# Two transformer layers and a third block on one core: layer boundaries rebuilt tile by tile, gate columns computed inside the layer, context first

## Chip, core and metric

One core of one Trainium2 chip, device time in microseconds (us), everything in fp32. Engines: PE (TensorE), DVE (VectorE), ACT (ScalarE), POOL (GpSimd), SP (SyncE, which here only issues the weight transfers). The change is judged by the median of three runs.

## What is computed

The input x has 256 tokens of 1024 numbers. Two layers follow that share their form, then a block of another form with a mixture of 16 experts. Cut to the parts that matter here:

```python
for l in range(2):                                   # the two layers
    shift, scale, gate = split3(silu(c) @ w_ada[l] + b_ada[l])
    h = rms_norm(x, g_pre[l]) * (1 + scale) + shift
    y = sum of three gated attention branches over h, then @ w_out[l]
    x = x + gate * rms_norm(y, g_post[l])
# second block: shift1, scale1, gate1, shift2, scale2, gate2 = silu(c_2) @ w_mod_2 + b_mod_2
h  = rms_norm(x,   g_pre1_2) * (1 + scale1) + shift1
hc = rms_norm(ctx, g_pre1_2) * (1 + scale1_ctx) + shift1_ctx     # 256 context tokens
x = x + gate1 * rms_norm(windowed and recurrent attention over hc and h @ w_out_2, g_post1_2)
x = x + gate2 * rms_norm(sum over experts e of scatter(w_down[e] @ act(w_gate[e], w_up[e])), g_post2_2)
```

Shift, scale and gate are called the columns: each is a vector of 1024 numbers per condition, made from 4 MB of weights in six pieces of 512 for one layer (pieces 0 to 3 are shift and scale, 4 and 5 the gate).

## The kernel before

The kernel is written by hand: each engine has its own instruction stream, and semaphores count what is done. Work on PE is a list of **jobs**, each of which fills one of three PSUM banks in turn (job j uses bank j mod 3); the next user of a bank waits until ACT or DVE has read it (`reader`, `free`, `taken`). `layer_jobs` and `second_jobs` are these lists, in order. Weights come through a ring of 6 slots of 1 MB, filled by SP in the order of `layer_loads` and `second_loads`. A load waits for the last job that uses the load six places ahead of it, and SP issues strictly in order.

Jobs that the text names. `xT`, `xT2`, `cT`: transposes of normalised x or context, evicted with scale and shift into hT or hcT by ACT (even) and DVE (odd). `ada`, `mod`: 512 columns of a conditioning product; `modT`: their turn onto partitions, after an ACT copy, reduced by DVE. `gate`: gate columns spread over partitions, read by DVE into G1. `cq`, `ckv`, `qb`, `kb` and so on: projections of hT. `wo`, `wout`: output projections; wout has four jobs of 8 products of 128x512, two for each tile of 128 tokens. In the second block `tq`, `tk`, `tkc` are queries, keys and context keys, `rq`, `rk` the rotations of q and k, `nv` values.

Order of a layer: 4 xT, 3 gate, cq ckv qb kb, small projections; 24 attention units, between which the *fill* jobs (z, g, ada, modT) are spread by `share`; 12 wo; 4 wout. Then the **boundary**: DVE copies the four wout banks to SBUF, ACT squares the copies, DVE and POOL make the inverse root, DVE scales by G1 and adds to x for both tiles, ACT issues three small loads (lvecs, b_ada, g_post) and squares x, POOL makes the root, DVE normalises both tiles, and PE transposes. The columns for layer l+1 are made in the fill of layer l, all six pieces, and those for layer 0 in the prologue, ahead of the loop (`FIRST_MODS`). The two layers are one hardware loop (`Fori`). Ahead of the prologue's columns PE computes bias tables (L711, L715), which go to DRAM and come back skewed (t_rows, na_rows). The second block starts with loads of context, constants (consts2) and gate rows once x is done.

The experts' weights, 16 times about 33 MB, stream through a ring of 13 slots; at the end ACT squares the four output tiles, DVE scales, adds, and SP stores x.

## Time and profile before

| | us |
|---|---|
| median of 3 runs | 2490.72 (2490.24 to 2492.41) |
| profiled execution, its own time | 2487.14 |
| its span, first to last instruction | 2484.7 |
| PE busy | 1887.4 (76%) |
| DVE busy | 511.9 (21%) |
| ACT busy | 284.8 (11%) |
| DMA | 714.89 MB, mean 288 GB/s |

Busy shares are means over stages of different kinds; PE's weight loads (PEld) overlap its products. A row of a timeline merges neighbouring instructions of one line, and the brackets at its end give the idle time of the engine before it and what ended that.

### The profile page before, as it was taken

Reading aid. Unit: us, or ns where it says so; the run is one execution under the profiler, and the core shown is the slowest. Engines: PE = TensorE matmul, PEld = TensorE weight load, DVE = VectorE, ACT = ScalarE, POOL = GpSimd, SP = SyncE. Lnnn points to the kernel's source line nnn. Section 1 sums busy time; section 2 is a strip of 40 time slices with the busy share of each in tenths; the row PEclk is TensorE's granted clock in tenths of the full one; section 3 lists DMA queues with packets and bytes.
Section 4 is the critical chain, followed back from the end, with each engine's and each line's share of the span. In section 5 each row is a group of like instructions: output and inputs, shape, how many; then the busy total and the mean of one; then the engine's idle time right before and its main releaser. Section 6 shows DMA issues by size and latency. Waiting matters only on the chain.

```text
span 2484.7 us, 25429 instructions
## 1 busy us (share of the span) xinstructions
PE 1887.4 (76%) x10486; PEld 1043.9 (42%) x10486; DVE 511.9 (21%) x1131; ACT 284.8 (11%) x699; POOL 53.1 (2%) x80
## 2 busy tenths in 40 slices
PE   5899999799999699977656666666666666666665
PEld 1767776668777567533412222222222222222221
DVE  1224322224322226743300000000000000100001
ACT  1112220113220112311100000000000000000000
POOL 0000000000000300020000000000000000000000
PEclk9999999899999899999788878887788788878787
DMA  9633563233554411156599999999999999999996
GB/s 322 185 136 107 199 220 120 85 131 141 198 182 163 154 68 68 68 179 240 243 423 422 422 422 423 422 422 421 423 423 422 422 423 423 421 423 422 423 423 274
DMA packets 149549, 714.89 MB, mean 288 GB/s; under 512 B 11711, under 2 KB 16191, under 8 KB 95904
## 3 DMA queue, kind: packets, MB, share of 16 engines
q1 hardware_dynamic: 143776, 697.08, 70.0%
q0 software_dynamic: 2016, 7.21, 1.2%
q10 hardware_dynamic: 3640, 8.94, 1.1%
q8 instruction: 86, 1.41, 0.2%
q14 instruction: 31, 0.25, 0.0%
HBM read 709.38 MB, written 3.80 MB: 287 GB/s over the span
## 4 chain that ended last, share of the span: by engine, by line
issue 64%; PE 29%; DVE 4%; DMA 2%; ACT 1%; POOL 0%; ACTq 0%; POOLq 0%; DVEq 0%
PE banks L756 10%; PE banks L1539 3%; PE banks L1548 3%; PE banks L761 1%; PE banks L810 1%; PE banks L1584 1%; PE banks L1569 1%; PE banks L876 1%; DVE arena L2015 1%; PE banks L819 1%; PE banks L715 1%; PE banks L904 1%; DMA arena<-in_w_mods_dram 1%; PE banks L886 1%; DVE arena L1945 1%
## 5 line engine op out<-in xcount | busy, mean ns | idle before, releaser
L2231 PE MATMUL banks<-arena 128*32 128x512 f32 (+2 forms) x3072 | 468.1, 739 | 307.0 <-DMA arena<-in_w_up_dram 301.1
L2231 PEld LDWEIGHTS banks<-arena 128*32 128x32 f32 x3072 | 128.5, 136 | 587.4 <-issue 580.8
L756 PE MATMUL banks<-arena 128*128 128x256 f32 x1536 | 344.8, 382 | 1.4 <-DVE arena L1253 1.4
L756 PEld LDWEIGHTS banks<-arena 128*128 128x128 f32 x1536 | 289.3, 191 | 43.0 <-DVE arena L1253 3.2
L2258 PE MATMUL banks<-arena 128*32 128x512 f32 x1280 | 212.9, 803 | 114.6 <-DMA arena<-in_w_down_dram 75.5
L2370 DVE SCALAR_TENSOR_TENSOR arena<-arena,banks 64x512 f32<-64x512 f32 (+1 forms) x48 | 30.5, 635 | 787.9 <-ACT arena L2283 787.2
L2258 PEld LDWEIGHTS banks<-arena 128*32 128x32 f32 x1280 | 46.7, 132 | 261.5 <-issue 260.1
L2283 ACT ACTIVATE arena<-banks 64x512 f32<-64x512 f32 (+1 forms) x48 | 26.6, 555 | 837.6 <-PE banks L2231 831.7
L1539 PE MATMUL banks<-arena 128*128 128x256 f32 x512 | 113.4, 380 | 0.2 <-DVE arena L1880 0.2
L1539 PEld LDWEIGHTS banks<-arena 128*128 128x128 f32 x512 | 96.3, 191 | 12.9 <-DVE arena L1880 0.4
L2377 DVE COPY arena<-banks 128x512 f32<-128x512 f32 x16 | 11.1, 692 | 369.1 <-PE banks L2266 369.1
L848 PE MATMUL banks<-arena 128*128 128x256 f32 x384 | 83.4, 380 | 1.3 <-DVE arena L1349 1.3
L848 PEld LDWEIGHTS banks<-arena 128*128 128x128 f32 x384 | 73.0, 191 | 11.8 <-issue 2.2
L1548 PE MATMUL banks<-arena 128*128 128x512 f32 x160 | 69.7, 594 | 1.1 <-DVE arena L1909 1.1
L2203 PE MATMUL banks<-arena 128*128 128x512 f32 x128 | 60.9, 619 | 0.8 <-ACT arena L2297 0.8
L2235 PE MATMUL banks<-arena 128*32 128x128 f32 x512 | 60.2, 316 | 0.0
L856 PE MATMUL banks<-arena 128*128 128x512 f32 x128 | 55.4, 594 | 3.1 <-issue 3.1
L2235 PEld LDWEIGHTS banks<-arena 128*32 128x32 f32 x512 | 37.7, 133 | 36.7 <-issue 21.8
L2297 ACT COPY arena<-banks 128x512 f32<-128x512 f32 x16 | 9.4, 585 | 344.7 <-PE banks L2266 344.7
L2214 PE MATMUL banks<-arena 64*128 64x64 f32 x176 | 30.4, 296 | 21.7 <-DVE arena L2372 13.0
L1051 ACT ACTIVATE arena<-arena 128x256 f32<-128x256 f32 x64 | 32.0, 500 | 125.6 <-DVE arena L1275 67.0
L1548 PEld LDWEIGHTS banks<-arena 128*128 128x128 f32 x160 | 30.2, 191 | 37.9 <-issue 36.0
(316 smaller groups left out, 1657.9 us busy)
## 6 DMA issues: line engine op xcount, KB each, us to landing
arena<-in_w_gate_dram SPq DMA_DIRECT2D x128, 1376.0 KB, 30.1
arena<-in_w_up_dram SPq DMA_DIRECT2D x128, 1376.0 KB, 31.9
arena<-in_w_down_dram SPq DMA_DIRECT2D x160, 1024.0 KB, 30.4
arena<-in_w_in_dram SPq DMA_DIRECT2D x68, 1024.0 KB, 7.2
arena<-in_w_mods_dram SPq DMA_DIRECT2D x48, 1024.0 KB, 7.3
arena<-in_w_out_dram SPq DMA_DIRECT2D x12, 1024.0 KB, 5.1
arena<-in_w_down_dram SPq DMA_DIRECT2D x16, 512.0 KB, 21.7
arena<-in_w_o_swa_dram SPq DMA_DIRECT2D x4, 1024.0 KB, 10.5
```

Source lines behind the costliest of these rows:

```text
L756: mm = pe.matmul(b[:, i * S:i * S + S], w, rhs[:, kt, :], start=kt == 0, stop=kt == 7)
L848: mm = pe.matmul(b[:, i * S:i * S + S], w[:, k, c:c + P], zv[:, 4 * br + k, :], start=k == 0, stop=k == 3)
L856: mm = pe.matmul(b, hTv[:, kt, t * P:t * P + P], slot(loads[0] + kt // 4)[:, kt % 4, :], start=kt == 0, stop=kt == 7)
L1051: ins = nc.scalar.activation(Ev[:, u % 3, t * S:t * S + S], src, ACT.Exp, bias=nmx[:, u % 3, t:t + 1], scale=QK ** -0.5 if kind == "mla" e ...
L1539: mm = pe.matmul(b[:, i * S:i * S + S], slot(loads[kt // 4])[:, kt % 4, c0:c0 + P], rhs[:, kt, :], start=kt == 0, stop=kt == 7)
L1548: mm = pe.matmul(b, lhs[:, kt, (n % 2) * P:(n % 2) * P + P], slot(loads[kt // 4])[:, kt % 4, :], start=kt == 0, stop=kt == 7)
L2203: mm = pe.matmul(acc[2 * t + c], GT[:, e % 2, t * P:t * P + P], Y[:, 512 * c:512 * c + 512], start=e == 0, stop=e == NE - 1, skip_group_ch ...
L2214: mm = pe.transpose(MB[:, b:b + 64], hid[0:64, c], ident[0:64, 0:64])
L2231: mm = pe.matmul(bank[pc][32 * g:32 * g + 32, 0:w_], xsT[:, kt, CAP * e4:CAP * e4 + CAP], (wg if g < 2 else wu)[:, c:c + w_], start=kt == ...
L2235: mm = pe.matmul(bank[pc][32 * g:32 * g + 32, LAST - c0:w], xsT[:, kt, CAP * e4:CAP * e4 + CAP], (wg if g < 2 else wu)[:, FF - 64:FF].unsq ...
L2258: mm = pe.matmul(bank[c][32 * g:32 * g + 32, :], hTv3[:, j, 32 * hf:32 * hf + 32], w_[:, 512 * c:512 * c + 512], start=(g, c) not in start ...
L2370: nc.vector.scalar_tensor_tensor(h_, h_, 1.0, bank[pc][0:64, 0:w], ALU.add, ALU.mult).then_inc(own3.sem, own3.up())
```

## The change

At each boundary y stays in PSUM: ACT squares the wout banks directly, DVE scales them from PSUM by a G1 that already holds the factor 0.5, and each tile of 128 tokens goes its own way, from the sum of squares to the transposes. wout runs tile by tile. Shift and scale of the next stage are computed in the fill as before (4 pieces instead of 6); the gate's two pieces are loaded and computed inside the layer they belong to, and in the second block inside that. Gate jobs move among the middle projections. Small loads of the next stage are issued after the last attention unit, in the last layer also those of the context, which is squared and normalised there. The second block starts with context keys. In the prologue the constants load first, table products stand between column products, and the layers are unrolled. At the end scaling, addition and stores go by tile and half.

```diff
@@ layer_loads, layer_jobs @@
     chunk("w_in", D, COL["qb"], 512)
+    for c in (4, 5):
+        chunk("mods_now", D, 512 * c, 512)
     chunk("w_in", D, COL["kb"], 256)
...
-    for c in range(3):
-        jobs.append(("gate", c, ()))
...
-    jobs += [("qb", 0, (i, i + 1)), ("qb", 1, (i, i + 1))]
-    i += 2
+    jobs += [("qb", 0, (i, i + 1)), ("ada", 4, (i + 2, i + 3)), ("qb", 1, (i, i + 1)), ("ada", 5, (i + 4, i + 5)), ("modT", 4, ())]
+    i += 6
...
-    for c in range(2):
-        jobs += [("wout", 2 * c, (i, i + 1)), ("wout", 2 * c + 1, (i, i + 1))]
-        i += 2
+    for t in range(2):
+        jobs += [("wout", 2 * t + c, (i + 2 * c, i + 2 * c + 1)) for c in range(2)]
+    i += 4
@@ prologue @@
-FIRST_MODS = [("ada", 0), ("ada", 1), ("modT", 0), ("ada", 2), ("modT", 1), ("ada", 3), ("modT", 2), ("ada", 4),
-              ("modT", 3), ("ada", 5), ("modT", 4), ("modT", 5)]
+FIRST_MODS = [("ada", 0), ("ada", 1), ("modT", 0), ("ada", 2), ("modT", 1), ("ada", 3), ("modT", 2), ("modT", 3)]
@@ second_loads, second_jobs @@
-ORDER2 = ("qn", "kn", "vn", "qh", "zf", "zb", "gh", "ih")
+ORDER2 = ("kn", "vn", "qn", "qh", "zf", "zb", "gh", "ih")
...
-    jobs = [("xT2", i, ()) for i in range(4)] + [("cT", i, ()) for i in range(4)]
-    jobs += [("gate2", i, ()) for i in range(3)]
+    jobs = [("cT", i, ()) for i in range(4)]
...
+    jobs += [("tkc", n, i["kn"]) for n in range(2)]
+    jobs += [("xT2", n, ()) for n in range(4)]
+    jobs += [("own", 4, i["own", 4]), ("own", 5, i["own", 5])]
+    jobs += [("tk", n, i["kn"]) for n in range(2)]
+    jobs += [("ownT", 4, ()), ("ownT", 5, ())]
+    jobs += [("nv", n, i["vn"]) for n in range(2)] + [("gate2", n, ()) for n in range(3)]
+    jobs += [("rk", n, ()) for n in range(2)] + [("nv", n, i["vn"]) for n in (2, 3)]
+    jobs += [("tq", n, i["qn"]) for n in range(2)] + [("rq", n, ()) for n in range(2)]
@@ PE @@
-            with pe.Fori(0, LAYERS) as l:
+            for l in range(LAYERS):
@@ ACT, end of a layer @@
+                for t in range(2):
+                    for c in range(2):
+                        n = 2 * t + c
+                        j = JOB_OF["wout", n]
+                        act.wait_ge(job_done.sem, made(l, j))
+                        nc.scalar.activation(E[:, 512 * n:512 * n + 512] if n < 3 else th[:, 0:512], bank[j % BANKS], ACT.Square,
+                                             scale=0.5, accum_out=s4[:, n:n + 1]).then_inc(ysq.sem, ysq.up())
+                    act.wait_ge(xup.sem, xup.at(l, t + 1))
+                    nc.scalar.activation(xnv[:, t, :], xv[:, t, :], ACT.Square, accum_out=xss[:, t:t + 1]).then_inc(xsq.sem, xsq.up())
@@ DVE, end of a layer @@
-                for t in range(2):
-                    nc.vector.scalar_tensor_tensor(xnv[:, t, :], xnv[:, t, :], rs[:, t:t + 1], G1, ALU.mult, ALU.mult).then_inc(v_own.sem, v_own.up())
+                    for c, j in enumerate(js):
+                        a = slice(512 * c, 512 * c + 512)
+                        nc.vector.scalar_tensor_tensor(xnv[:, t, a], bank[j % BANKS], rs[:, t:t + 1], G1[:, a],
+                                                       ALU.mult, ALU.mult).then_inc(reader(j), 1)
...
+                    nc.vector.tensor_tensor(xv[:, t, :], xv[:, t, :], xnv[:, t, :], ALU.add).then_inc(xup.sem, xup.up())
+                    x_mean(l + 1, t)
+                    x_scale(l + 1, t)
```

What stands on PE at the start, before (L711 and L715 are the bias tables, L729 the column products, L735 their turns):

```order
L711 MATMUL banks<-arena 12x512
L715 MATMUL banks<-arena 120x512 x8
L729 MATMUL banks<-arena 32x512 x16
L735 MATMUL banks<-arena 128x128 x4
L729 MATMUL banks<-arena 32x512 x8
```

and after (L751 column products, L757 turns, L761 and L740 tables, L818 xT, L789 cq and ckv):

```order
L751 MATMUL banks<-arena 32x512 x16
L757 MATMUL banks<-arena 128x128 x4
L761 MATMUL banks<-arena 12x512
L740 MATMUL banks<-arena 120x512 x4
L751 MATMUL banks<-arena 32x512 x8
L757 MATMUL banks<-arena 128x128 x4
L740 MATMUL banks<-arena 120x512 x4
L751 MATMUL banks<-arena 32x512 x8
L757 MATMUL banks<-arena 128x128 x8
L818 MATMUL banks<-arena 128x128 x16
L789 MATMUL banks<-arena 128x256 x24
```

The tables moved behind the first column products, two column products and two turns are gone, and nothing stands between xT and cq.

DVE at the end of layer 0, before (L1385 scales by G1, L1387 adds to x, both on whole tiles):

```order
L1382 TENSOR_SCALAR arena<-arena 128x2
L1383 REGISTER_ALU
L1385 SCALAR_TENSOR_TENSOR arena<-arena 128x1024
L1386 REGISTER_ALU
L1387 TENSOR_TENSOR arena<-arena 128x1024
L1385 SCALAR_TENSOR_TENSOR arena<-arena 128x1024
L1386 REGISTER_ALU
L1387 TENSOR_TENSOR arena<-arena 128x1024
```

and after (L1468 scales from PSUM, L1472 adds, L1210 and L1214 are the mean and the normalising of x for the next layer, L1255 evicts xT):

```order
L1461 TENSOR_TENSOR arena<-arena 128x1
L1463 TENSOR_SCALAR arena<-arena 128x1
L1468 SCALAR_TENSOR_TENSOR arena<-banks,arena 128x512 x2
L1472 TENSOR_TENSOR arena<-arena 128x1024
L1210 TENSOR_SCALAR arena<-arena 128x1
L1214 TENSOR_SCALAR arena<-arena 128x1024
L1461 TENSOR_TENSOR arena<-arena 128x1
L1463 TENSOR_SCALAR arena<-arena 128x1
L1468 SCALAR_TENSOR_TENSOR arena<-banks,arena 128x512 x2
L1472 TENSOR_TENSOR arena<-arena 128x1024
L1210 TENSOR_SCALAR arena<-arena 128x1
L1214 TENSOR_SCALAR arena<-arena 128x1024
```

The steps of one tile now follow each other, up to its normalising, before those of the next.

PE at the start of the second block, before (L1527 xT2 and cT, L1520 gates, L1539 projections of keys and queries, L1544 rotations, L1548 nv, L1603 first scores):

```order
L1527 MATMUL banks<-arena 128x128 x32
L1520 MATMUL banks<-arena 128x128 x8
L1539 MATMUL banks<-arena 128x256 x96
L1544 MATMUL banks<-arena 128x512 x4
L1548 MATMUL banks<-arena 128x512 x32
L1603 MATMUL banks<-arena 128x256 x4
```

and after (L1620 cT, L1633 projections, L1611 xT2, L1592 own columns, L1599 their turns, L1642 nv, L1605 gates, L1638 rotations, L1698 first scores):

```order
L1620 MATMUL banks<-arena 128x128 x16
L1633 MATMUL banks<-arena 128x256 x32
L1611 MATMUL banks<-arena 128x128 x16
L1592 MATMUL banks<-arena 32x512 x16
L1633 MATMUL banks<-arena 128x256 x32
L1599 MATMUL banks<-arena 128x128 x8
L1642 MATMUL banks<-arena 128x512 x16
L1605 MATMUL banks<-arena 128x128 x8
L1638 MATMUL banks<-arena 128x512 x2
L1642 MATMUL banks<-arena 128x512 x16
L1633 MATMUL banks<-arena 128x256 x32
L1638 MATMUL banks<-arena 128x512 x2
```

The first scores come next there, so the rotations of q are the last work ahead of them; before, the values were.

## Rows read from the trace of the kernel before

**Rows 1.** The page: tenths busy and GB/s in 40 slices of the span.
```profile
PE   5899999799999699977656666666666666666665
GB/s 322 185 136 107 199 220 120 85 131 141 198 182 163 154 68 68 68 179 240 243 423 422 422 422 423 422 422 421 423 423 422 422 423 423 421 423 422 423 423 274
```

**Rows 2.** Stretches: length, busy (count) of PE, PEld, DVE, ACT, POOL, clock, DMA share, GB/s.
```profile
248.00:310.00 62.00, 60.31 (x331) 47.69 (x320) 22.53 (x68) 16.93 (x50) 2.79 (x4) 1.00 0.55 202
431.00:449.00 18.00, 0.89 (x3) 0.09 (x2) 8.48 (x15) 3.11 (x7) 1.39 (x2) 0.62 0.40 127
```

**Rows 3.** PE's waits up to 1290 us: total, times, longest.
```profile
PE banks L789 <- DVE arena L1188: 31.5, 2, 17.1
PE banks L1527 <- DMA arena<-in_consts_dram: 18.7, 1, 18.7
```

**Rows 4.** Timeline of PE, 0 to 90 us: start, duration, instructions, idle before.
```profile
10.05 1.88 PE L711 MATMUL banks<-arena 33*12 33x512 f32 x2 [10.05 <-DMA arena<-in_na_hot_dram]
11.85 14.00 PE L715 MATMUL banks<-arena 32*120 32x512 f32 x16
...
27.59 6.13 PE L729 MATMUL banks<-arena 128*32 128x512 f32 x32 [1.73 <-DVE arena L1151]
34.24 1.92 PE L729 MATMUL banks<-arena 128*32 128x512 f32 x16
...
68.77 3.68 PE L789 MATMUL banks<-arena 128*128 128x128 f32 x16 [14.43 <-DVE arena L1188]
75.06 14.19 PE L761 MATMUL banks<-arena 128*128 128x256 f32 x64 [0.21 <-DVE arena L1205]
```

**Rows 5.** DMA: page totals; windows 40:45, 20:25 (two rows), 16:28; issues, time to landing.
```profile
q1 hardware_dynamic: 143776, 697.08, 70.0%
q0 software_dynamic: 2016, 7.21, 1.2%
...
DMA packets 976, 1.93 MB, mean 387 GB/s; under 512 B 32, under 2 KB 32, under 8 KB 976
...
DMA packets 428, 1.01 MB, mean 203 GB/s; under 512 B 19, under 2 KB 19, under 8 KB 428
q1 hardware_dynamic: 342, 0.66, 34.2%
...
q1 hardware_dynamic: 1193, 2.38, 51.6%
...
t_rows<-arena POOLq DMA_DIRECT2D x1, 768.0 KB, 13.5
na_rows<-arena POOLq DMA_DIRECT2D x1, 1920.0 KB, 20.4
```

**Rows 6.** Timeline between the two layers, DVE and PE.
```profile
434.79 1.28 DVE L1385 SCALAR_TENSOR_TENSOR arena<-arena 128x1024 f32<-128x1024 f32 x1
...
448.92 3.68 PE L789 MATMUL banks<-arena 128*128 128x128 f32 x16 [17.11 <-DVE arena L1188]
454.83 14.19 PE L761 MATMUL banks<-arena 128*128 128x256 f32 x64 [0.44 <-DVE arena L1205]
```

**Rows 7.** Timeline of PE at the start of the second block.
```profile
832.02 3.74 PE L1527 MATMUL banks<-arena 128*128 128x128 f32 x20 [18.75 <-DMA arena<-in_consts_dram]
...
837.70 2.05 PE L1520 MATMUL banks<-arena 128*128 128x128 f32 x16 [0.18 <-DVE arena L1867]
839.95 41.71 PE L1539 MATMUL banks<-arena 128*128 128x256 f32 x192 [0.20 <-DVE arena L1880]
```

**Rows 8.** The same timeline, from the values to the first scores.
```profile
886.93 27.73 PE L1548 MATMUL banks<-arena 128*128 128x512 f32 x64 [1.05 <-DVE arena L1909]
915.44 1.14 PE L1603 MATMUL banks<-arena 64*128 64x256 f32 x8 [0.78 <-ACT arena L1683]
```

**Rows 9.** Issue to landing of the second block's weight loads of 1 MB (L1488).
```profile
DMA to landing us min/median/max: 5.0/7.4/11.6
```

**Rows 10.** Timeline at the end: the last scatter.
```profile
2469.04 3.67 PE L2203 MATMUL banks<-arena 128*128 128x512 f32 x8 [0.84 <-ACT arena L2297]
```

More of the change, by code:

```diff
@@ L1120, in _ @@
             pool.dma_start(scr_na, EN[0:120, :]).then_inc(na_out, 16)
-            pool.wait_ge(const_in, 32)
-            minus_half = C("half")
-            with pool.Fori(0, LAYERS) as l:
+            for l in range(LAYERS):
                 enter("pool", l)
@@ L1237, in _ @@
                 dve.wait_ge(reader(j), taken(l, j))
+                columns(5)
+                dve.wait_ge(rows_in, 32 * l + 32)
                 for kind, n, _ in MIDDLE:
-                    if kind not in ("kc", "rotq"):
+                    if kind not in ("kc", "rotq", "gate"):
                         continue
@@ L1242, in _ @@
                     dve.wait_ge(job_done.sem, made(l, j))
+                    if kind == "gate":
+                        a = slice(3 * P * n, min(D, 3 * P * n + 3 * P))
+                        nc.vector.tensor_tensor(row_b[:, a], bank[j % BANKS][:, 0:a.stop - a.start], row_b[:, a], ALU.add).then_inc(v_own.sem, v_own.up())
+                        dve.wait_ge(v_own.sem, v_own.last())
+                        nc.vector.scalar_tensor_tensor(G1[:, a], row_b[:, a], 0.5, row_g[:, a], ALU.mult, ALU.mult).then_inc(reader(j), 1)
+                        continue
                     if kind == "kc":
@@ L1330, in _ @@
                         if kind == "modT":
[L1331 to L1333 removed]
+                            columns(n)
                         if kind == "z":
@@ L1530, in job @@
                     ctx_ = kind == "tkc" or (kind in ("zf", "zb") and n < 2)
-                    if kind == "tq" and n == 0:
-                        for jj in range(JOB2["xT2", 3] - 2, JOB2["xT2", 3] + 1):
+                    if kind in ("tkc", "tk") and n == 0:
+                        for i in range(4):
+                            jj = JOB2["cT" if kind == "tkc" else "xT2", i]
                             pe.wait_ge(reader(jj), taken(L2, jj))
@@ new lines, in _ @@
+            for n in range(2):
+                j = JOB2["tkc", n]
+                dve.wait_ge(job_done.sem, made(L2, j))
+                nc.vector.tensor_copy(kc2[:, 512 * n:512 * n + 512], bank2(j)).then_inc(reader(j), 1)
+            for t in range(2):
+                j = JOB2["xT2", 2 * t + 1]
+                dve.wait_ge(job_done.sem, made(L2, j))
+                for i in range(4):
+                    ins = nc.vector.tensor_scalar(hTv[:, 4 + i, t * P:t * P + P], bank2(j)[:, i * P:i * P + P],
+                                                  AB1[0][:, 12 + i:13 + i], AB1[0][:, 4 + i:5 + i], ALU.mult, ALU.add)
+                ins.then_inc(reader(j), 1)
```

574 lines of the change are left out of this document (309 added, 265 removed).

## Prediction, made blind

> **What bounds the kernel now.** I read the page first: TensorE (PE) is busy in nine tenths or more of most slices of the first half, and from slice 21 on the DMA engines are full at 422 GB/s while PE falls to six tenths [rows 1]. The stretch table says the same: in 248 to 310 us, an attention stage, PE works 60.31 of 62 us [rows 2]. The second half is a stream of expert weights of fixed size, so it is neither lengthened nor shortened: whatever is won before it moves it earlier by as much. The first half pays one for one wherever PE waits, and the list of PE's waits gives the places: 31.5 us in two waits of the transposes L789, 18.7 us in one of L1527 [rows 3]. These are the boundaries the change rewrites. The timeline says how they are made. At the start PE runs table products and the columns' products until 54 us, then idles 14.4 us, and the first real projection (cq, L761) starts at 75.06 [rows 4]. Between the layers PE has ended 17.11 before it transposes at 448.92, so at 431.8, and reaches cq at 454.83: 23.0 us [rows 6]. Before the second block it has ended 18.75 before 832.02, at 813.3, and starts tq at 839.95: 26.7 us [rows 7].
>
> **Start.** The four loads and two products for gate columns leave the prologue, the table products fill PE's gaps, small loads and gates leave its path. Two limits remain. PE alone: about 10 us until constants are in (estimated from 10.05, where the first table product could start), two column products 6.1, two more 2 x 1.92, four turns of columns 2.6, table products 1.9 + 14.0, transposes 3.7, a last eviction about 1.2 [rows 4]: 43. The transfers: before cq 8.4 MB of column weights, 1.7 MB of w_in and 2.35 MB of small loads must land, 12.5 MB. The undisturbed rate is 1.93 MB in 5 us, 387 GB/s; while the bias tables are written the weights get 0.66 MB in 5 us [rows 5]. In the 13.5 us that this write takes to land [rows 5] the weights move 1.8 MB, the remaining 10.7 take 27.6 us, start-up 2.5: 43.6. But the skewed reads and the na_rows write, which came after 63 us, now start as the last table product ends, about 37 us. At the shared rate of 198 GB/s (2.38 MB in the 12 us from 16 to 28 [rows 5]) the 2.9 MB then outstanding take 15 us: 51. Because cq starts on the first half of its weights I take **48** (bounds 43 and 52): 75.1 - 48 = **27** us gained.
>
> At the rate question stands the Trainium skill, DMA: Bandwidth & Descriptors, section Queues, rings and completion order: each DMA engine takes turns between queues, a packet at a time. With mean packets of 4.85 KB (weights) and 3.58 KB (tables), from the page's queue totals [rows 5], weights would keep 58% of 387, 222 GB/s, cq would be bound by PE at 44 and the whole sum would be 4 us lower. This speaks for the change, as a rival below. The row shows 131 with the total down to 203 GB/s [rows 5], so here the measurement does not agree.
>
> **Inside each layer.** PE's work is the same: six column products before, two for this layer and four for the next after. The fill between attention units gets shorter by 5.2 us (products 2 x 1.92 [rows 4], turns about 0.66 each), at no cost as long as PE is what bounds there (60.31 of 62 [rows 2]); were VectorE's chain the bound, up to 5 us per layer would not come back. The gates' 2.0 us [rows 7] move from the boundary into the middle: -2.0 per layer. A load waits for the last user of its slot, six loads back, and SP issues in order: kb's weights now wait for qb 1. 1 MB, which is what kb's two loads hold, landed after 5.0 us at best [rows 9]; covered by ada 5 (1.92 [rows 4]) and some 1.7 for a turn and the spread of the root, it leaves **1** us (0 to 3) per layer. In the first layer the own column weights (4 MB) arrive while the tables travel: **2** us (0 to 8). Start in all: 27 - 2 - 1 - 2 = **22**.
>
> **Between the layers.** Tile 0's chain runs under wout 2 and 3, each as long as a job nv (27.73 for four [rows 8]: 6.9). Tile 1's remains after PE's end. In 431 to 449 us VectorE worked 8.48, ScalarE 3.11 and POOL 1.39 us for both tiles [rows 2]. Of ScalarE's, 0.8 is the square of a quarter and 1.15 that of a tile: 2.0 remain. POOL's two roots remain, 1.4. Of VectorE's, the copy (0.7) goes and of scaling, addition and normalising (1.28 [rows 6], 1.2 and 0.75 a tile) one tile's remain, halved scaling costing 0.1 more: 3.3, with 0.6 of small steps. Hand-overs 0.6: 7.9 us. Then xT 2 and 3, 0.92 each at the low clock (3.68 for four [rows 6]), and the eviction in four pieces of 128x128, which no row has: the whole eviction of the four old jobs lay within the 5.9 us from 448.92 to 454.83, so it is below 2.2 (5.9 less 3.7), and not below 1.0 (half the columns of 0.5 for 128x256); I take 1.2 and 0.2 to start it, near the lower end, since the columns are halved: cq at +11.2. 23.0 - 11.2 = 11.8, less gates and kb: **8.8**. The granted clock after the wait was the low level (0.62 in the stretch table) [rows 2] and may be so again; included above.
>
> **Before the second block.** Context is normalised under wout. After PE's end: 7.9 of chain; then VectorE, in order, does the lbs steps (0.6) and the evictions of cT 1 and 3 (1.0 each): tkc starts at +10.7. From there to the first scores PE's work adds up: three pairs of projections (tkc, tk, tq; 64 of the 192 products in 41.71 each) 41.7; xT2 2.4, between the 3.68 of 16 transposes at the low clock and half of it; the own columns 3.8 and their turns 1.2; four jobs nv 27.7; gates 2.05; rotations 3.5 [rows 4, 7, 8]: 82.4. New waits: vn's two loads sit in kn's slots, and kn is used last by tk 1, so they issue only when that ends; the first lands 5.0 later at best [rows 9], with the two turns (1.2) as cover: **3.8** (3 to 7). Behind this wait stand nv, the gates and everything up to the scores. The rotations of q come last, so the first scores wait for six VectorE steps of 0.72 (3.7 beyond PE's own 1.7 and the hand-over), which nv used to cover: **3.7** (2 to 5). A bank that the gates hold costs 0.2. 10.7 + 82.4 + 7.7 = 100.8, against 915.44 - 813.3 = 102.2 now: **1.4**. So the 16 us that the shorter chain gives here go three ways: 5.0 for the columns moved in from the prologue (there they count as gained), 4.4 for xT2 and gates that stood in the old 26.7, and 5.3 net of waits (7.7 new, 2.4 old).
>
> **End.** Squares of the four tiles start as each product ends instead of after all (3.67 us for four) and the last square ends about 1.5 us earlier; the last transfer follows a 128x512 addition rather than 128x1024 (1.22 us) and is half as big. VectorE still does all of its closing work, about 5 us [rows 10]: **2.2**.
>
> **Sum.** 22 + 8.8 + 1.4 + 2.2 = 34.4. The profiled execution took 2487.1 us (span 2484.7), so 2452.7; it stood 3.6 below the runs' median 2490.7, which gives **2456** for the median.
>
> **Rivals.**
> - Table traffic or the own columns hold the start (12%): cq at 52 and 8 us of waits for own columns instead of 2: 10 us worse, 2466. For it: 20.4 us to land na_rows, 203 GB/s while tables travel [rows 5]. Against: the tables' own volume is the same as before, and most of the weights behind them have a stage of 14 us to arrive in.
> - The shorter fill is missed (8%): 5 us a layer do not come back, 2466. Against: PE idle of 1.7 us in 62 [rows 2].
> - The waits in the second block are longer and drop the clock (10%): 7 + 5 in place of 3.8 + 3.7, and 1.7 lost at the low level: 2462.
> - Everything hides, and the unrolled layers shed the register steps ahead of waits (17%): cq at 43, no wait for kb or own columns, 3 us of steps: 5 + 2 + 2 + 3, 2444.
> - The other side (2%): the two layers are unrolled, and PE's instructions are fetched instead of looped over. From 75 to 813 us are 738 us; it decides once PE there runs 34.4 us, or 4.7%, longer. At 10% it is 74 - 34 = 39 us slower than now, 2530. Against: the expert part is straight-line code already, and its DMA is full all the time [rows 1]. No change at all would need the same coincidence (1%).
> - Weights keep the larger share of the engines beside the tables (5%): 222 GB/s, by the packet sizes of the two queues, instead of 131 to 198. Then PE's own 44 binds cq: 4 better, 2452. It is the Trainium skill's rule above. Against: the measured 0.66 MB in 5 us [rows 5].
> - My forecast (45%), its own range 2449 to 2463.
>
> **Numbers.** Cases within reach run from 2444 to 2466; the single bounds reach further (cq's start -5 or +4, own columns +6, kb +4, fill +10, the second block's waits +5). Not all at once: 2442 to 2471. Faster by over 0.2% (5 us, about what can be told from no change) 0.97, the same 0.01, slower 0.02.
>
> **What would show it.** Right: cq at 44 to 52 us; PE's gap between layers in two pieces, together near 9 us instead of 17.1; tkc about 11 us after the last wout; a wait for w_in near 4 us at nv 0, one for VectorE near 4 us at the first scores, and 101 us from the last wout to them; the expert stage still at 422 GB/s and equally long. Wrong: over 8 us of waits for w_mods in layer 0, PE below 58 of 62 us in the attention stages, or a last stage that starts earlier but is longer.

## The result and the profile after

The changed kernel takes 2466.55 us in the median of 4 runs (2465.06 to 2471.28) against 2490.48 of before on the same chip (4 runs, 2489.96 to 2492.41): ratio 0.9906, 95% interval 0.9889 to 0.9923, 23.9 us faster. The forecast was 2456 against 2490.7, that is 34.4 faster; the size is 10 us short. The profiled execution has a span of 2463.2 us, 21.5 less than before. Of run 3 below one execution took 2941.10 us, at a mean granted clock of 0.63, and is left out of its median.

The start, PE's timeline (start, duration, instructions, idle before), to be read against [rows 4]:

```profile
9.56 1.94 PE L751 MATMUL banks<-arena 128*32 128x512 f32 x8 [9.56 <-DMA arena<-in_w_mods_dram]
17.87 1.94 PE L751 MATMUL banks<-arena 128*32 128x512 f32 x8 [6.37 <-DMA arena<-in_w_mods_dram]
20.69 1.94 PE L751 MATMUL banks<-arena 128*32 128x512 f32 x8 [0.89 <-DMA arena<-in_w_mods_dram]
23.31 1.94 PE L751 MATMUL banks<-arena 128*32 128x512 f32 x8 [0.68 <-DMA arena<-in_w_mods_dram]
...
26.22 1.88 PE L761 MATMUL banks<-arena 33*12 33x512 f32 x2
28.03 7.18 PE L740 MATMUL banks<-arena 32*120 32x512 f32 x8
35.13 3.64 PE L751 MATMUL banks<-arena 128*32 128x512 f32 x16
...
43.97 3.64 PE L751 MATMUL banks<-arena 128*32 128x512 f32 x16
...
54.06 14.17 PE L789 MATMUL banks<-arena 128*128 128x256 f32 x64 [1.66 <-DVE arena L1255]
...
79.19 1.07 PE L801 MATMUL banks<-arena 128*32 128x512 f32 x8 [0.59 <-DMA arena<-in_w_mods_dram]
81.78 1.06 PE L801 MATMUL banks<-arena 128*32 128x512 f32 x8 [1.52 <-DMA arena<-in_w_mods_dram]
```

The reader is to see that PE does nothing for 9.56 us and little until 20, waiting for column weights, and only at 26 begins the tables, whose inputs landed by 16 us at the latest (run 3 below). The first projection, L789, starts at 54.06 instead of 75.06. The products themselves are slow here: eight of L751 take 1.94 us, eight of L801, of the same form, 1.07 at 79.19. The clock column doesn't show this at first: it reads 1.00 for 35.1 to 38.7 us and 0.50 for 44.0 to 47.5, and 16 products take 3.64 us in both. So the durations decide. The list of PE's waits in the first 54 us sums it up (total, times, longest):

```profile
PE banks L751 <- DMA arena<-in_w_mods_dram: 17.5, 4, 9.6
```

The last of these waits ends at 23.31 us. The write of the table rows, the first of the table traffic, is issued by POOL only then:

```profile
37.15 0.90 POOL L1163 DMA_DIRECT2D t_rows<-arena  x1
```

Between the layers, where [rows 6] had one gap of 17.11 us:

```profile
387.71 27.70 PE L884 MATMUL banks<-arena 128*128 128x512 f32 x64 [1.77 <-DVE arena L1438]
...
417.99 0.65 PE L818 MATMUL banks<-arena 128*128 128x128 f32 x4 [2.14 <-DVE arena L1468]
422.85 1.94 PE L818 MATMUL banks<-arena 128*128 128x128 f32 x8 [4.21 <-DVE arena L1214]
```

The last wout ends at 387.71 + 27.70 = 415.41; the gap is now 2.14 (a bank that DVE still reads), 4.21 (the chain of tile 1) and 1.66 before cq, which starts at 426.45.

The second block, against [rows 7] and [rows 8]; L1620 is cT, L1633 the projections tkc, tk, tq, L1642 the values nv, L1698 the scores:

```profile
790.49 1.31 PE L1620 MATMUL banks<-arena 128*128 128x128 f32 x8 [2.14 <-DVE arena L1468]
794.57 1.12 PE L1620 MATMUL banks<-arena 128*128 128x128 f32 x4 [2.76 <-ACT arena L1774]
797.62 16.94 PE L1633 MATMUL banks<-arena 128*128 128x256 f32 x64 [1.94 <-DVE arena L1931]
...
820.76 14.08 PE L1633 MATMUL banks<-arena 128*128 128x256 f32 x64
...
840.51 15.67 PE L1642 MATMUL banks<-arena 128*128 128x512 f32 x32 [4.79 <-DMA arena<-in_w_in_dram]
...
860.19 13.89 PE L1642 MATMUL banks<-arena 128*128 128x512 f32 x32
...
893.33 2.08 PE L1698 MATMUL banks<-arena 64*128 64x256 f32 x8 [3.56 <-DVE arena L1984]
895.34 5.54 PE L1633 MATMUL banks<-arena 128*128 128x256 f32 x16
```

Two things are to be seen. The announced waits are there, 4.79 for vn's weights and 3.56 for VectorE before the first scores. And equal work differs in length: 64 products take 16.94 us behind the boundary and 14.08 later, 32 values 15.67 and 13.89, a score row 2.08 where [rows 8] has 1.14. The granted clock tells why (stretches; after the counts: clock, DMA share, GB/s):

```profile
422.00:432.00 10.00, 7.49 (x22) 6.04 (x23) 4.43 (x14) 2.21 (x7) 0.00 (x0) 0.53 0.06 20
432.00:440.00 8.00, 8.00 (x38) 6.62 (x37) 0.00 (x0) 0.77 (x2) 0.00 (x0) 1.00 0.00 0
794.00:804.00 10.00, 7.49 (x20) 5.91 (x21) 2.88 (x8) 1.43 (x4) 10.00 (x17) 0.53 0.37 126
893.00:900.00 7.00, 6.67 (x21) 5.11 (x22) 3.65 (x10) 0.81 (x2) 0.00 (x0) 0.57 0.30 113
```

0.53 means nearly all at the lower of the two levels (1.2 GHz), 1.00 the upper (2.4). PE had idled ahead of each low stretch: 4.21 and 1.66 us ahead of the first, 2.76 and 1.94 around the second, 3.56 ahead of the third.

The end: the squares of the four output tiles start as each product ends (2451.96 to 2454.54), where they had waited for all, and the span closes 12.37 us after the last scatter starts, in place of 15.66.

Stage by stage, in us, before and after from the same kinds of row; "won" is positive where the changed kernel is faster.

| stage | before | after | won | forecast |
|---|---|---|---|---|
| to cq of layer 0 | 75.06 | 54.06 | 21.0 | 27 |
| layer 0, cq to end of wout | 356.7 | 361.3 | -4.6 | -5 |
| end of wout to cq of layer 1 | 23.0 | 11.0 | 12.0 | 11.8 |
| layer 1, cq to end of wout | 358.4 | 361.5 | -3.0 | -3 |
| end of wout to first scores | 102.2 | 105.4 | -3.2 | 1.4 |
| first scores to the first expert product | 301.6 | 305.2 | -3.7 | 0 |
| expert products to the last scatter | 1252.1 | 1252.3 | -0.2 | 0 |
| last scatter to the end | 15.7 | 12.4 | 3.3 | 2.2 |
| sum (spans differ by 21.5) | | | 21.6 | 34.4 |

Three terms are short: the start by 6.0, the second block by 4.6, the stage behind it by 3.7, in all 14.3. The middle of the kernel came within 0.5 us a term, and the end gave 1.1 more. 14.3 less 1.1 and the small ones is the 12.8 that is missing in the sum. In medians 10.5 are missing: the profiled execution of before stood 3.6 us below its median, that of after 1.5.

### The profile page after: what moved, and what is told of

Same layout as the page of the kernel before. It is cut to its first block, busy times and chain, and to the rows that moved or that the text cites. A ratio compares the mean times of both kernels' runs of the same rounds, so it can differ in the third digit from the quotient of the medians.

```text
span 2463.2 us, 24454 instructions
## 1 busy us (share of the span) xinstructions
PE 1898.9 (77%) x10486; PEld 1042.2 (42%) x10486; DVE 510.6 (21%) x1148; ACT 287.7 (12%) x711; POOL 55.5 (2%) x86
## 4 chain that ended last, share of the span: by engine, by line
DMA 38%; PE 36%; DVE 5%; ACT 1%; issue 1%; SPq 1%; POOL 0%; DVEq 0%; ACTq 0%
DMA arena<-in_w_up_dram 33%; PE banks L784 7%; PE banks L2313 6%; DMA arena<-in_w_down_dram 4%; PE banks L1633 4%; PE banks L1642 3%; PE banks L2340 2%; PE banks L876 2%; PE banks L2282 2%; PE banks L1678 1%; PE banks L884 1%; PE banks L1663 1%; DVE arena L2090 1%; PE banks L2267 1%; PE banks L904 1%
## 5 line engine op out<-in xcount | busy, mean ns | idle before, releaser
L1633 PE MATMUL banks<-arena 128*128 128x256 f32 x512 | 118.5, 391 | 1.9 <-DVE arena L1931 1.9
L1633 PEld LDWEIGHTS banks<-arena 128*128 128x128 f32 x512 | 99.3, 197 | 17.9 <-issue 4.3
L1642 PE MATMUL banks<-arena 128*128 128x512 f32 x160 | 71.5, 605 | 4.8 <-DMA arena<-in_w_in_dram 4.8
L1642 PEld LDWEIGHTS banks<-arena 128*128 128x128 f32 x160 | 30.7, 194 | 42.2 <-issue 41.7
```

Source lines behind the costliest of these rows:

```text
L1633: mm = pe.matmul(b[:, i * S:i * S + S], slot(loads[kt // 4])[:, kt % 4, c0:c0 + P], rhs[:, kt, :], start=kt == 0, stop=kt == 7)
L1642: mm = pe.matmul(b, lhs[:, kt, (n % 2) * P:(n % 2) * P + P], slot(loads[kt // 4])[:, kt % 4, :], start=kt == 0, stop=kt == 7)
```

## The experiments

Two theories stood at the outset. **Serial start, uncovered waits, idle clock**: the start is PE's waits and work in series, the second block's two waits come from job order, and the low clock comes from PE's idling. **The rival**: transfers and table traffic bound the start, the load queue is late at vn anyway, and the low clock belongs to the place or the chip. Each run was timed beside the kernel before; medians over different chips are comparable to some 2 us (before stood at 2490.3 to 2492.3). Runs 1 to 4 were on one chip, 5 to 8 on a second, 9 to 11 on a third, 12 on a fourth; the changed kernel was timed only for the result. So "less than the changed kernel" carries these 2 us, and for runs 1, 5 and 9 the intervals of the ratios overlap its own (0.9889 to 0.9923): what these show is read from their rows.

### 1. tk ahead of the own column products

```diff
-    jobs += [("own", 4, i["own", 4]), ("own", 5, i["own", 5])]
     jobs += [("tk", n, i["kn"]) for n in range(2)]
+    jobs += [("own", 4, i["own", 4]), ("own", 5, i["own", 5])]
```

> The changed kernel with tk moved ahead of the layer's own column products in the second block, nothing else. Theory (the wait for vn's weights is the time from the end of tk 1 to the landing less what PE has to do meanwhile): the cover grows from the two turns (1.2 us) to the two products and the turns (5.0), so the wait of 4.79 us for a DMA at nv 0 falls to 0 to 1, and the first scores start 4 to 5 us sooner after the last wout (105.4 -> about 101); the whole 2462 against 2466.5. If PE keeps its clock through there, another 1 to 2 us. Rival (the weights are late because the queue in front of them is late, not because of their issue): the wait stays over 3 us wherever it stands, and the time is 2466.

2463.37 us, ratio 0.9893 (0.9877 to 0.9909), 3.2 less.

```profile
819.45 14.05 PE L1633 MATMUL banks<-arena 128*128 128x256 f32 x64 [1.55 <-DVE arena L1943]
...
839.11 13.97 PE L1642 MATMUL banks<-arena 128*128 128x512 f32 x32 [0.60 <-DMA arena<-in_w_in_dram]
```

The wait for vn falls from 4.79 to 0.60, so it was a matter of cover. But tk now follows the transposes at once and waits 1.55 us for the eviction that the own products had covered. From tkc to the first scores 91.7 us instead of 95.7: 4.0 won. The chain from a transposed tile through its eviction was missing in the expectation. And nv 0 and 1, behind 0.60 us of idle time instead of 4.79, take 13.97 us instead of 15.67.

### 2. tq and rq ahead of the last values

```diff
-    jobs += [("rk", n, ()) for n in range(2)] + [("nv", n, i["vn"]) for n in (2, 3)]
-    jobs += [("tq", n, i["qn"]) for n in range(2)] + [("rq", n, ()) for n in range(2)]
+    jobs += [("rk", n, ()) for n in range(2)]
+    jobs += [("tq", n, i["qn"]) for n in range(2)] + [("rq", n, ()) for n in range(2)]
+    jobs += [("nv", n, i["vn"]) for n in (2, 3)]
```

> The changed kernel with tq and the rotations of q placed ahead of nv 2 and 3, nothing else. Theory: the 3.56 us for which PE waits for VectorE before the first scores are the rotation's steps, laid bare because nothing follows them on PE; with 6.9 us of nv behind them the wait falls under 0.5 us. The low granted clock in the first scores (16 products L1633 at 5.54 us in all instead of 3.72, and L1698 2.08 instead of 1.14) follows that idle time and goes with it, 2 to 3 us more. The vn wait before nv 0 stays (4.8). Sum 5.5 to 6.5: 2460.5 against 2466.5. Rival (clock and wait are unconnected, the low clock belongs to that place in the program): only 3.5 us come back, 2463, and the first attention products stay at 5.5 us.

2460.74 us, ratio 0.9878 (0.9863 to 0.9892), 5.8 less.

```profile
891.17 1.13 PE L1699 MATMUL banks<-arena 64*128 64x256 f32 x8 [0.78 <-ACT arena L1767]
892.24 3.72 PE L1634 MATMUL banks<-arena 128*128 128x256 f32 x16
```

The wait is 0.78, as short as in [rows 8] (it is ACT's copy of the last values, not none), and the scores and products behind it take 1.13 and 3.72 instead of 2.08 and 5.54. So 3.56 us of idle time cost 2.8 us more in the clock. The rival, a low clock tied to the place, is out here. (Run 8 below keeps the wait of 3.56; there the same rows take 1.87 and 4.62, which is 1.6 more and not 2.8.)

### 3. Tables first, and 4. the same with the table rows sent late

```diff
+            pe.wait_ge(tables_in, 64)
+            pe.matmul(MB[0:12, :], TAB[0:33, 0:12], T5[0:33, :], start=True, stop=True).then_inc(pro_pe.sem, pro_pe.up())
+            bias_tables(0, 4)
             pe.wait_ge(const_in, 32)
...
+                if (kind, c) == ("ada", 0):
+                    bias_tables(4, 6)
                 if (kind, c) == ("modT", 0):
+                    bias_tables(6, 8)
@@ only in run 4, POOL @@
+            pool.wait_ge(job_done.sem, made(0, JOB_OF["ada", 5]))
             pool.dma_start(scr_t5, T5S[0:12, :].unsqueeze(1).to_broadcast([12, 32, REL])).then_inc(t5_out, 16)
```

> The changed kernel with the table products ahead of and between the column products in the prologue (T5 and four bias tables before column product 0, two after it, two after turn 0), VectorE's copies in the same order, nothing else. Theory (the start is PE's serial waits and work: it waits for weights first, 17.5 us in four pieces, and does the tables only after): the tables fill those waits, the last column product comes when its weights have landed (33.4 us) and cq starts at 42 to 47 instead of 54.06; a part of the 7 to 12 us may be eaten by weights of cq and by own columns that now wait for the table rows' write: 2456 to 2461, in the middle 2458. Rival (transfers bound the start): cq does not start before 51, 2464 or more.

> As the run with the tables first, and the write of the rows t_rows (and with it the skewed reads and the write of na_rows) is held back until the second own column product of layer 0 has been made; its source is another buffer so that nothing waits for it. It tells how much of the start belongs to table traffic. If it does not bind: the same cq start as in the run with the tables first within 1 us, and own-column waits of layer 0 of 2 us or less in both. If it does: cq 3 to 8 us sooner than in that run, and the waits for weights in layer 0 (2.1 + 0.6 us in the changed kernel) gone. Serial theory expects 2456, at most 2 us under the other run; the rival 5 us or more under it.

Both were misses: 2474.00 us, ratio 0.9931 (0.9912 to 0.9950), and 2480.22, 0.9956 (0.9943 to 0.9969), 7.5 and 13.7 us slower than the changed kernel. Run 3:

```profile
16.12 1.88 PE L741 MATMUL banks<-arena 33*12 33x512 f32 x2 [16.12 <-DMA arena<-in_na_hot_dram]
...
49.56 14.17 PE L789 MATMUL banks<-arena 128*128 128x256 f32 x64 [1.83 <-DVE arena L1254]
...
84.44 1.94 PE L801 MATMUL banks<-arena 128*32 128x512 f32 x8 [7.66 <-DMA arena<-in_w_mods_dram]
```

Run 4:

```profile
50.66 14.17 PE L789 MATMUL banks<-arena 128*128 128x256 f32 x64 [1.66 <-DVE arena L1253]
...
76.82 1.92 PE L801 MATMUL banks<-arena 128*32 128x512 f32 x16
...
106.10 2.08 PE L952 MATMUL banks<-arena 128*128 128x128 f32 x8 [17.81 <-POOL arena L1175]
```

The changed kernel loads the tables' inputs behind constants and x, so they come at 16.12, and tables that now stand first begin late. cq still starts 4.5 us sooner, but the second half of an own column product waits 7.66 us while the skewed reads and na_rows travel with its weights. In run 4 POOL, which also makes the inverse root of the latent norms, stood in its queue behind the rows that I had held back: PE waited 17.81 us for it. Its total therefore says nothing on transfers, but its start does, as its expectation had set out. POOL sends the table rows at 88.45 us here and at 40.94 in run 3, and cq starts at 50.66 against 49.56: without the traffic it is no sooner (the tables' inputs landed at 17.27 for 16.12, which is the difference), so table traffic doesn't hold cq. And the own column products wait for nothing (76.82), so the 7.66 us of run 3 were table traffic.

### 5. Unread products in PE's waits

```diff
+            def warm(k):
+                for _ in range(k):
+                    pe.matmul(SB[0][:, 0:S], ident, cst[:, 0:S], start=True, stop=True)
...
+                        if l > 0:
+                            warm({0: 4, 2: 9}.get(n, 0))
                         pe.wait_ge(xn_ready.sem, xn_ready.at(l, t + 1))
```

(and 3 before cq, 12 around cT and tkc, 7 before the scores; each product is two rows of the trace)

> The changed kernel with 35 matmuls added whose result nobody reads (constants times the identity, 128x256, 0.43 us each at the high clock, 0.87 at the low one, 128x256 written to a bank of the scores): 16 between the layers, 12 before the context keys, 7 before the first scores, all in places where PE waits, none longer together than the wait that follows. Theory (the low granted clock behind the boundaries, 16.62 and 16.94 us for jobs of 14.1 and 13.9, 15.67 for nv 0 and 1, 5.54 for 16 products that take 3.72, is what PE's idling ahead of it brings): PE's projections after the boundaries take 14.1 and 13.9 again, the waits themselves stay: 5 to 9 us less than 2466.5, so about 2460. Rival (the low clock comes from something else, such as power of the whole chip, or the time when it falls is the chip's own): the low stretches move but their sum stays, 2466 and up to 2 more because dummies at the low clock outlast a wait.

2463.01 us, ratio 0.9887 (0.9871 to 0.9903), 3.5 less in the median where 5 to 9 were expected; the profiled execution was the fastest of the four, 2455.83, and the other three (2462.24 to 2464.95) left no trace. L737 are the added products, L793 cq, L1645 tkc:

```profile
418.97 4.15 PE L737 MATMUL banks<-arena 128*128 128x256 f32 x18
...
425.85 14.17 PE L793 MATMUL banks<-arena 128*128 128x256 f32 x64
...
794.56 14.05 PE L1645 MATMUL banks<-arena 128*128 128x256 f32 x64 [1.10 <-DVE arena L1945]
...
887.16 1.14 PE L1712 MATMUL banks<-arena 64*128 64x256 f32 x8 [0.54 <-DVE arena L1998]
```

cq takes 14.17 where it took 16.62, tkc 14.05 where it took 16.94. nv 0 and 1 stay at 15.48, behind their uncovered wait of 4.77. So the low clock follows idle time at three places and goes with it, and work without use keeps the high one. The three places give back 8.1 us in this trace (2.4, 2.9 and 2.8); why the median gives only 3.5 is open.

### 6. The kernel before with its layers written out

```diff
-            with pe.Fori(0, LAYERS) as l:
+            for l in range(LAYERS):
```

(the same on all five engines)

> The kernel before with its register loop over the two layers written out by Python's loop on all five engines, nothing else: the part of the change that moves no work. Prediction's main case: no change, 2490.7 within 2 us. The rival in which written-out layers shed the register steps ahead of waits: 2 to 3 us less (2488). The rival in which PE's instructions are then fetched too slowly: 20 us and more longer, and PE's layers 5 to 10% longer.

2491.22 us against 2491.54, ratio 0.9997 (0.9988 to 1.0007). In the kernel before unrolling costs nothing and gives nothing that can be told; both rivals that rested on it are out.

### 7. Tables first, loads and POOL's queue in order

```diff
@@ ACT @@
-            act.dma_start(vv, A["vecs"]).then_inc(const_in, 16)
-            act.dma_start(cst, A["consts"]).then_inc(const_in, 16)
-            act.dma_start(xv, A["x"][0].rearrange("(t p) d -> p t d", p=P)).then_inc(x_in, 16)
             act.dma_start(TAB[0:33, 0:12], A["t5_tab"]).then_inc(tables_in, 16)
...
+            act.dma_start(vv, A["vecs"]).then_inc(const_in, 16)
...
@@ POOL @@
+            def send_tables():
+                pool.wait_ge(job_done.sem, made(0, JOB_OF["ada", 5]))
...
                 root(1, rs4, ms4)
+                if l == 0:
+                    send_tables()
```

(send_tables holds POOL's old lines for t_rows, the skewed reads and na_rows)

> The tables first, done without the two faults of the runs before: the tables' own inputs are loaded first again (they landed at 16.1 us behind the constants and x in the run with the tables first, at 10.05 in the kernel before), and POOL sends t_rows, the skewed reads and na_rows after its first root and after the second own column product of layer 0, so that no root stands behind them (17.8 us of PE's time in the run with late rows) and they take no transfer time from the own columns (7.66 us of wait in the run with the tables first). Theory (start = serial waits and work of PE): cq at 43 to 46 us, own-column waits at most 2 us, the whole about 2456 (2453 to 2460, the granted clock at the boundaries being worth up to 4 us either way). Rival (transfers hold the start whatever PE does): cq at 49 or later and own-column waits of 4 and more: 2464.

2460.28 us, ratio 0.9879 (0.9864 to 0.9894).

```profile
10.09 1.88 PE L741 MATMUL banks<-arena 33*12 33x512 f32 x2 [10.09 <-DMA arena<-in_na_hot_dram]
...
19.05 3.64 PE L753 MATMUL banks<-arena 128*32 128x512 f32 x16
...
29.14 1.92 PE L753 MATMUL banks<-arena 128*32 128x512 f32 x16
...
33.13 1.06 PE L753 MATMUL banks<-arena 128*32 128x512 f32 x8 [0.48 <-DMA arena<-in_w_mods_dram]
...
40.29 15.84 PE L789 MATMUL banks<-arena 128*128 128x256 f32 x64 [1.66 <-DVE arena L1257]
```

PE works from 10 to 38 us almost without a wait and cq starts at 40.29, 13.8 us sooner than in the changed kernel and sooner than the 43 to 46 expected. This run also moves the table traffic behind cq, so it doesn't by itself tell order from transfers; run 4 does, and both together say that the start was a matter of order. The 13.8 us have two parts of one size. PE's waits up to cq are 13.5 us instead of 20.2, and its products take 27.7 us instead of 34.6, though they are the same: from 22 us on 16 column products take 1.92 us, where they took 3.64 to 3.88 in the changed kernel. But only 7.6 us of it reach the attention stage (first scores there at 157.35, in the changed kernel 164.90): PE waits 5.0 us for weights at kb, qc and kc, which now meet the table traffic, where it had waited 2.1 for own columns and 0.55 at kb; that is 2.4 more, and cq and qb at the low clock take 1.7 more each. The whole is at the upper end of the 2453 to 2460 expected.

### 8. One own column product in PE's gap

```diff
-    jobs = [("cT", i, ()) for i in range(4)]
+    jobs = [("own", 4, (0, 1))] + [("cT", i, ()) for i in range(4)]
```

(with its weights ahead of kn, own 5's behind them, and ACT's copy ahead of its wait for x)

> The changed kernel with one of the second block's two own column products (4) moved into PE's gap ahead of the context's transposes, its weights loaded ahead of the keys'; vn's weights then wait for that product's slots and issue right after the last wout. Theory: the product (1.9 us) fills the first of the boundary's waits (2.14), and the wait of 4.79 us before nv 0 goes: 5.5 to 6.7 us less, 2460.5; and PE's idle time there falls, so that the clock may stay high. Rival (the load queue is behind by then whatever the order, or the context keys now wait for weights that come 2.4 us later per load): tkc waits for w_in for 1 us or more, and the whole is 2464 or more.

2459.83 us, ratio 0.9872 (0.9855 to 0.9888), 6.7 less.

```profile
834.76 13.98 PE L1648 MATMUL banks<-arena 128*128 128x512 f32 x32
```

nv follows without a wait at 834.76 instead of 840.51; the boundary waits become 0.72, 2.33 and 2.40, tkc waits for its evictions and not for weights. Two things act here: the product fills 1.4 of the first wait, and vn's weights, issued sooner, take away the wait of 4.79 and with it the low clock of nv 0 and 1 (13.98 for 15.67).

### 9. The table traffic split

```diff
@@ against run 7, in send_tables @@
-                pool.wait_ge(job_done.sem, made(0, JOB_OF["ada", 5]))
...
+                pool.wait_ge(job_done.sem, made(0, JOB_OF["kc", 1]))
                 pool.dma_start(scr_na, EN[0:120, :]).then_inc(na_out, 16)
```

> As the run with the tables first and the queue clear, but t_rows and the skewed reads go right after POOL's first root (57.9 us there, a stretch of 106 GB/s in which the own columns had already landed), and the write of na_rows waits until kc 1 has been made. There cq started at 40.29 us but 4.4 us of waits for w_in came back at qc and kc, behind table traffic of 80 to 116 us. Theory (the table traffic costs whatever weights have to be landed beside it, wherever it stands, and nothing in a stretch where the queue is idle): cq at 40 to 41, waits for w_in and w_mods between 60 and 140 us under 2 us in all instead of 5.1, 3 us less than the 2460.3 of that run: 2457. Rival (the cost is conserved: own columns or kb now wait 3 us and more): 2460.

2464.11 us, ratio 0.9897 (0.9880 to 0.9915), 3.8 more than run 7 (on another chip, and the intervals overlap): a miss, and the rival's 3 us and more for kb came true. cq starts at 40.62, and kb waits 8.91 us, where run 7 has 0.66. What travels in its stretch, 74 to 88 us (queue: packets, MB, share; q0 the table traffic, q1 the weights):

```profile
DMA packets 961, 2.75 MB, mean 197 GB/s; under 512 B 64, under 2 KB 449, under 8 KB 961
q0 software_dynamic: 576, 2.36, 82.1%
q1 hardware_dynamic: 385, 0.39, 13.4%
```

The weights get 0.39 of 2.75 MB. They move 385 packets against 576, but the mean packet is 1.0 KB against 4.1, since kb's rows are 256 numbers. The Trainium skill, DMA: Bandwidth & Descriptors, section Queues, rings and completion order, says that each engine changes queues packet by packet; with whole turns, and with the profile's packets counted as those of the page, the weights would have had half of the packets and, at 1.0 KB each, a fifth of the bytes. The trace agrees in kind: two packets in five, a seventh of the bytes. In the prediction I set this rule aside on [rows 5], where weights of larger packets got 131 GB/s. Here it fits that kb, of all loads, starves; that the packet size is the cause no run shows, since none changes it.

### 10 and 11. All together, without and with the unread products

Run 10 joins the edits of runs 9, 8 and 2. Run 11 adds those of run 5, resized to the waits that run 8 leaves, 33 products in all (the expectation says 34):

```diff
+                warm({JOB2["cT", 0]: 1, JOB2["cT", 3]: 5, JOB2["tkc", 0]: 4}.get(j, 0))
```

> Start as in the run with the rows split, own product 4 in PE's gap (with vn's weights early), and tq and rq ahead of nv 2 and 3. By the single runs against 2466.5: start 6.3 and 3 more, own in gap 6.7, rq early 5.8 of which up to 2 are clock: sum 20 to 22, 2445 to 2447. If they overlap (the clock's share counted twice): 2450.

> The same with the 34 unread matmuls in PE's waits at the two boundaries and before the first scores. The single run gave 3.5 us in the median (9.2 in its profiled execution). Theory (idle time ahead brings the low clock): jobs of cq in layer 1 and tkc at 14.1 and 13.9 us in place of about 16.5, 3 to 6 us less than the run without. Rival (the low stretches only move elsewhere, for example into the expert part's start): the same time within 1 us, though the jobs behind the boundaries are short.

2449.40 us (2448.87 to 2452.92), ratio 0.9834 (0.9821 to 0.9848), and 2446.09 (2443.26 to 2448.03), 0.9820 (0.9806 to 0.9833), on one chip and with ranges that do not touch: the unread products are worth 3.3 us, within the 3 to 6 expected. Run 10 missed its 2445 to 2447, which counted 9.3 for the start; run 9 gave 2.4. With that the single gains don't overlap: 2.4 (run 9), 6.7 (8) and 5.8 (2) make 14.9, and 17.2 were measured, which is equal within the 2 us of different chips. The stretches 775 to 845 us, run 10 and then run 11:

```profile
775.00:845.00 70.00, 64.42 (x259) 41.84 (x258) 14.21 (x33) 11.46 (x26) 21.97 (x36) 0.95 0.59 180
```

```profile
775.00:845.00 70.00, 68.24 (x297) 45.99 (x297) 15.92 (x39) 10.92 (x25) 20.98 (x35) 1.00 0.61 180
```

### 12. The best placement of each

```diff
@@ against run 11, in send_tables @@
+                pool.wait_ge(job_done.sem, made(0, JOB_OF["ada", 5]))
                 pool.wait_ge(pro_v.sem, pro_v.at(0, 1))
```

> The run of everything with unread matmuls, with the table traffic placed otherwise: t_rows and the skewed reads after the second own column product (as in the run with the queue clear, where no own column and no kb weight waited for it), na_rows after kc 1 (as in the run with the rows split, where nothing waited for it). In the run with everything, kb waited 8.80 us for its weights behind t_rows and the skewed reads. Theory (table traffic takes from whatever weights are due beside it; qc's and kc's are due less urgently than kb's): kb waits under 1 us, qc and kc together 1 to 4 us, so 5 to 7 us less than 2446.1: 2440. Rival (conserved wherever it stands before the attention stage): the waits of qc and kc grow to 7 and more, 2445.

2442.09 us (2437.82 to 2444.21), ratio 0.9797 (0.9783 to 0.9810): 4.0 less than run 11, on another chip, and 24 less than the changed kernel. It lies between theory (2440) and rival (2445), and the waits decide. The three that remain for w_in:

```profile
78.12 3.69 PE L796 MATMUL banks<-arena 128*128 128x256 f32 x16 [0.82 <-DMA arena<-in_w_in_dram]
90.79 1.97 PE L791 MATMUL banks<-arena 128*128 128x256 f32 x8 [0.16 <-DMA arena<-in_w_in_dram]
95.78 5.45 PE L791 MATMUL banks<-arena 128*128 128x256 f32 x24 [3.02 <-DMA arena<-in_w_in_dram]
```

kb waits 0.82 us, the others 3.18 together: under 1 and 1 to 4, as theory had it, where run 11 had 8.80 for kb.

## Why the prediction was right, and where it was off

- **Bound and direction**: right. The expert stage is as long as before to 0.2 us, and what the first half won came out at the end less what its own stages gave back.
- **Start, 27 forecast, 21.0 measured**: the step that failed is "PE alone: about 10 us until constants are in", then its products, 43 in all; measured were 54.06. It let PE wait once and work from then on. The order rows show two column products ahead of the tables, and their weights landed in pieces: 17.5 us of waits for w_mods, 7.5 more than taken. It also priced the products by rows behind a busy PE: four column products 9.9 us, measured 15.0; turns 2.6, measured 3.7. Tables and transposes took 3.8 less than the 19.6 in the sum, and the waits around the transposes 1.5 more. The other limit, transfers at 51 (with 2.5 us of start-up that no row gives), had a wrong mechanism: PE's last wait for a transfer ended at 23.31 us, before the table traffic began at 37.15, and run 4, without that traffic, has cq no sooner than run 3. So 48 came near as a compromise between two limits of which neither held, which is luck. Runs 3, 4 and 7 also show that tables-first needs three orders to agree, PE's, ACT's loads and POOL's queue.
- **Layers, -5 and -3**: right, with kb 0.55 and 0.59 where 1 was taken, own columns 2.1 where 2 was taken. The fill is shorter at no cost, as PE's 60.31 of 62 us [rows 2] said.
- **Between the layers, 11.8**: 12.0. The chain took 2.14 and 4.21 with transposes between, cq came at +11.04 for +11.2. The low clock behind the gap, which I let stay as it was, cost cq of layer 1 2.4 us (16.62 against 14.19 in [rows 6]); it is inside layer 1's -3.0. There it is made up for by qb, whose 64 products took 15.75 us before and 14.32 after (1.4), by a kb wait of 0.59 for 1 (0.4), and by 0.6 that I can't place.
- **Second block, 1.4 forecast, -3.2 measured**: both new waits came in their places and near their sizes (4.79 for 3.8, 3.56 for 3.7; runs 1, 2 and 8 show that job order makes them). The mis-sized term is PE's 82.4 us: it used durations at the high clock behind two idle times. tkc 16.94 instead of 13.9 and nv 15.67 instead of 13.9 are 4.8 us, and nothing else of that size is missing (the chain was 1.0 shorter, 9.7 for 10.7, the two waits 0.9 longer).
- **Behind it, 0 forecast, -3.7**: scores and first products at the low clock, 2.8 us, shown by run 2. Of the rest 0.7 lies at the experts' lead-in, where 32 transposes behind idle time for the router take 6.34 us instead of 5.62; that was not tested.
- **End, 2.2**: 3.3. Of the 1.1 more, 0.8 is a wait of VectorE for POOL's root ahead of its first scaling, which stood in the old end and which the order by tile covers. Only the profile speaks for it; it had no run of its own.
- **Rivals**: unrolling is out (run 6). "The waits drop the clock" had 10% and a price of 1.7 us; the waits were not longer (4.79 and 3.56 where it had 7 and 5), but the drop of the clock was right and, with 7.6 us in the second block and behind it, more than four times as dear. "Table traffic or the own columns hold the start" (12%) had cq at 52 and 8 us of own-column waits: cq came at 54.06, for another reason, and the waits were 2.1. "Weights keep the larger share" needs table traffic beside the weights in the start, and there was none while PE waited. "The shorter fill is missed" is out: the layers gave what was forecast.

What stays open: how much the clock cost in the start, where its column doesn't show it and only durations do, and how long the low clock lasts behind a given idle time. cq of layer 1 took 16.62, 16.36, 16.82, 15.68 and 15.97 us in the changed kernel and runs 1, 3, 4 and 7 behind nearly the same waits. Nor is it shown what makes them differ. Differences of 1 to 3 us between whole kernels can come from that alone.

## What to carry over

A gap on PE has two prices: its length, and the low clock behind it; price the work behind each new wait at both levels, and fill gaps first with real work from elsewhere (run 8), then with anything (run 11). When an order changes on one engine, walk the same stretch on the engine that issues its loads and on the one whose queue holds small steps. Before adding up an engine's work at a start, set beside every piece the time at which its inputs land.

## What the runs showed of the hardware

Idle time of 3.56 us ahead of the scores cost another 2.8 us in clock (run 2), 1.6 in another kernel (run 8), and unread products in the waits gave 3.3 us over a whole kernel (runs 10 and 11). In the first 41 us of the changed kernel the clock column reads 1.00 while 16 column products take 3.64 us, as long as at 0.50 and nearly twice the 1.92 of run 7. Weights in 1.0 KB packets got a seventh of the bytes beside a queue of 4.1 KB packets (0.39 of 2.75 MB in 14 us, run 9). Writing two iterations of some 370 us each out straight changed the time by less than the measurement tells (0.9997, run 6).
